# Windowed means of a pooling mixer: sliding sums on VectorE over turned token tiles, in place of TensorE products with band and edge matrices

## The chip, the cores and the metric

The kernel runs on one core of one Trainium2 chip. The metric is the time of one execution on the device, in microseconds (us); for each kernel it is the median of its runs.

## What is computed

The reference is a two-layer decoder trunk over 1040 tokens (16 meta tokens ahead of 1024) of width 1024. Layer 0 mixes tokens with sparse attention and a gated recurrence, layer 1 with a causal pooling mixer. Behind each mixer comes a layer norm, then a SwiGLU block of width 2816, then another layer norm. The change touches the pooling mixer alone. Cut to what matters:

```python
POOL_WINDOWS = (2, 4, 8, 16)            # one window per group of 256 features
def multiscale_pool(h, w_pool, scale):
    cs = cumulative sum of h over the tokens, with a zero ahead
    for g, w in enumerate(POOL_WINDOWS):
        lo  = max(pos + 1 - w, 0)
        mean = (cs_g[1:] - cs_g[lo]) / (pos + 1 - lo)
        outs.append((mean - h_g) @ w_pool[g])       # 256 x 256
    return concatenate(outs) * scale

h = layer_norm(ALPHA * h + mix)
h = layer_norm(ALPHA * h + swiglu(h))
```

The 16 meta tokens are dropped from the output, so every token that is stored has a full window behind it, and the mean of a window of w is its sum over w.

## The kernel before, in words

Three stages follow one another: `projection`, `mixers` and `trunk`. The trunk is the SwiGLU blocks, the norms and the pooling mixer, and the change lies in it. The token tiles are tile 0 (the 16 meta tokens) and tiles 1 to 8 (128 tokens each); they stay in SBUF as `y`, with tokens on the partitions.

The trunk runs four phases: layer 0 for tiles 0 to 4, layer 0 for tiles 5 to 8, layer 1 for tiles 1 to 4, layer 1 for tiles 5 to 8. A phase has 11 pairs; a pair handles two slices of 128 hidden features. For each pair g, TensorE's program is: `gate_up(2g)` (48 products with a moving size of 512, L2067), `down(g-1)` (8 groups of 6 products, L2101), `gate_up(2g+1)`. Each fp32 weight is split into a high and a low part: ACT makes the high part (`high_w` L2181, `high_d` L2187), POOL the low part (`low_w` L1978, `low_d` L1985), the SP queue loads the next slice when both are done (`load_w` L1912). VectorE does `gated` (the product with the gate L2292, then the low part of the hidden values L2302) behind each `gate_up`, and `add` (L2318) behind each group of `down`. `down` turns over three PSUM banks: group n waits for the `add` of group n-3.

The norms and the pooling mixer of layer 1 lie between these pieces, written out by hand: `steps_in` says which token tile is in which step T in which pair. Phase 1 does it for tiles 1 to 4, phase 2 for tiles 5 to 8; one tile per pair, in eight pairs. For pooled tile j (tile m = j + 1):

- step T = j + 4: between `gate_up(2g)` and `down(g-1)`, `pool_d` (L2106) makes the windowed mean less the token, already turned so that features lie on the partitions. Eight products of a piece of `y` with a 128 x 128 `band` matrix (L2115), and eight with an `edge` matrix that bring in the last tokens of the tile before (L2121 for the first tile, L2124 else). ACT and VectorE copy the two PSUM banks out to `dT` (`turned_d`, L2211 and L2326), which has two buffers.
- step T = j + 5: behind the next pair's `down`, `pool_mix` (L2128) multiplies `dT` with the pooling weights (L2137), and VectorE adds the result to `y` and takes the norm's statistics (`mix`, L2329).
- step T = j + 8: `n2.turn` (L1764) turns the normed tile with eight TensorE transposes, between two `gate_up`s.

POOL makes `band` and `edge` in pairs 3 to 6 (`bands`, L1990), and keeps the tail of tile 4 for phase 2 (L2032). It multiplies the pooling weights with `pool_scale` in pair 8 (L2022).

An engine does its own instructions in the order in which they are written, and waits at semaphores.

Of the kernel before, what the change touches and what calls it, by code (L numbers as in the profile page):

```python
# [9 lines left out]
ALU = mybir.AluOpType  # L10
ACT = mybir.ActivationFunctionType

P = 128
D = 1024
# [1801 lines left out]
def trunk(nc, c, sem, sb, banks, ident, ins, y, hH, hL, raw, draw, out):  # L1816
# [3 lines left out]
    TAIL = 32  # L1820
# [17 lines left out]
    band = sb(c, "band", [P, NW, P])  # L1838
    edge = sb(c, "band_edge", [P, NW, P])
    dT = sb(c, "dT", [P, 2, DC, P])  # L1840
    meta_rest = dT[:, 1, :, :].rearrange("p k t -> p (k t)")
    scale = dT[:, 0, :, :].rearrange("p k t -> p (k t)").rearrange("p (g f) -> p g f", g=NW)
# [6 lines left out]
    pool_loaded, w_ready, made, made_all = sem("pool_loaded"), sem("pool_w"), sem("band_made"), sem("bands_done")  # L1849
    d_psum, d_act, d_dve, mix_psum, mixed, kept = (sem("d_psum"), sem("d_act"), sem("d_dve"), sem("mix_psum"),  # L1850
                                                   sem("mixed"), sem("tail_kept"))
# [18 lines left out]
    BANDS_AT = {3: 0, 4: 1, 5: 2, 6: 3}  # L1870
# [98 lines left out]
    def _(pool):  # L1969
# [18 lines left out]
        made_count = [0]  # L1988

        def bands(g):  # L1990
            win = POOL_WINDOWS[g]
            for mat, r, base in ((band, slice(0, P), 0), (edge, slice(0, N_META), N_META), (edge, slice(P - TAIL, P), TAIL)):
                at = mat[r, g, :]
                nc.gpsimd.memset(at, 1.0 / win).then_inc(made, 1)
                made_count[0] += 1
                pool.wait_ge(made, made_count[0])
                nc.gpsimd.affine_select(out=at, in_=at, compare_op=ALU.is_gt, fill=0.0, base=win - base,
                                        pattern=[[-1, P]], channel_multiplier=1).then_inc(made, 1)
                made_count[0] += 1
                pool.wait_ge(made, made_count[0])  # L2000
                if base == 0:
                    nc.gpsimd.affine_select(out=at, in_=at, compare_op=ALU.is_ge, fill=0.0, base=0,
                                            pattern=[[1, P]], channel_multiplier=-1).then_inc(made, 1)
                    made_count[0] += 1
                    pool.wait_ge(made, made_count[0])
                    nc.gpsimd.tensor_tensor(at, at, ident[:, :], ALU.subtract).then_inc(made_all, 1)

# [3 lines left out]
        for g in range(NPAIR):  # L2011
# [5 lines left out]
            if g in BANDS_AT:  # L2017
                bands(BANDS_AT[g])
            if g == SCALE_AT:
                pool.wait_ge(pool_loaded, 32)  # L2020
                for k in range(2):
                    nc.gpsimd.tensor_tensor(w[:, :, k, :], w[:, :, k, :], scale, ALU.mult).then_inc(w_ready, 1)  # L2022
            if first_norm(ph, i, 2) is not None:
                n0.bias(pool, first_norm(ph, i, 2))
            for T, normed, pooled in steps_in(ph, i):
                if T - 7 in pooled:
                    n2.bias(pool, T - 7)
                if T - 2 in normed:
                    n1.bias(pool, T - 2)
                    if T - 2 == HALF:  # L2030
                        pool.wait_ge(n1.biased, HALF + 1)
                        nc.gpsimd.tensor_copy(y[P - TAIL:P, 0, :], y[P - TAIL:P, HALF, :]).then_inc(kept, 1)  # L2032
                        pool.wait_ge(kept, 1)
# [9 lines left out]
    def _(pe):  # L2043
# [61 lines left out]

        def pool_d(j):  # L2106
            m = j + 1
            pe.wait_ge(n1.biased, m + 1)
            if j == 0:
                pe.wait_ge(made_all, NW)  # L2110
                pe.wait_ge(made, 3 * 2 * NW + NW)
            if m == HALF + 1:
                pe.wait_ge(kept, 1)
            for k in range(DC):
                nc.tensor.matmul(banks[:, PB + k // 4, k % 4 * P:(k % 4 + 1) * P], y[:, m, k * P:(k + 1) * P], band[:, k // 2, :],  # L2115
                                 start=(k % 4 == 0), stop=False)
            for k in range(DC):
                at = banks[:, PB + k // 4, k % 4 * P:k % 4 * P + N_META]
                cols, g = slice(k * P, (k + 1) * P), k // 2
                if m == 1:  # L2120
                    last = nc.tensor.matmul(at, y[0:N_META, 0, cols], edge[0:N_META, g, 0:N_META], start=False, stop=(k % 4 == 3))  # L2121
                else:
                    prev = 0 if m == HALF + 1 else m - 1
                    last = nc.tensor.matmul(at, y[P - TAIL:P, prev, cols], edge[P - TAIL:P, g, 0:N_META],  # L2124
                                            start=False, stop=(k % 4 == 3))
            last.then_inc(d_psum, 1)

        def pool_mix(j, turned):  # L2128
# [3 lines left out]
            pe.wait_ge(d_dve, d_made[0])  # L2132
            if turned:
                pe.wait_ge(n2.lo, 2 * turned)
            for g in range(NW):
                for k in range(2):
                    last = nc.tensor.matmul(banks[:, PB + g // 2, g % 2 * PG:(g % 2 + 1) * PG],  # L2137
                                            dT[:, j % 2, 2 * g + k, :], w[:, g, k, :], start=(k == 0), stop=(k == 1))
# [37 lines left out]
    def _(act):  # L2176
# [27 lines left out]

        def turned_d(j):
            act.wait_ge(d_psum, j + 1)
            if j == 0:
                act.wait_ge(w_ready, 2)
            if j >= 2:
                act.wait_ge(mix_psum, j - 1)  # L2210
# [223 lines left out]
```

## Time and profile before

| | us |
|---|---|
| median of 3 runs | 2550.95 (2549.44 to 2551.99) |
| the profiled execution, its own time | 2547.58 |
| its span, first to last instruction | 2545.9 |
| TensorE matmuls busy (share of the span) | 2469.9 (97%) |
| VectorE busy | 1114.2 (44%) |
| ScalarE busy | 950.1 (37%) |
| GpSimd busy | 1062.1 (42%) |
| mean granted TensorE clock, of full speed | 0.992 |

In the profile PE is TensorE's matmuls, PEld its weight loads, DVE is VectorE, ACT ScalarE, POOL GpSimd and SP the queue that issues the loads. A timeline row gives an instruction's start and its duration from the span's start; a bracket at its end is the idle time of the engine ahead of it and what ended that. Neighbouring matmuls overlap in the record, so the cost of one is the distance between two starts, not its duration. An fp32 product that is not a transpose is two instructions in the trace; `x16` is eight products.

### The profile page before, as it was taken

What the parts mean: (1) busy time and instruction counts of PE and PEld (TensorE: products, weight loads), DVE (VectorE), ACT (ScalarE), POOL (GpSimd) and SP (SyncE); (2) the same over time, 40 slices, a digit from 0 to 9 for tenths busy, and PEclk for the clock granted to TensorE, in tenths of its full rate; (3) what the DMA queues carried; (4) which work ended last, traced back from release to release, by engine and by line L of the source; (5) the groups of instructions that cost most, each with busy time, mean ns of one, the idle gap of its engine ahead of it and who ended that gap; (6) DMA issues with size and microseconds to landing.
All of it is one profiled execution on the core that took longest, in us unless ns stands there. A gap on an engine that the chain in (4) does not pass through costs nothing.

```text
span 2545.9 us, 36095 instructions
## 1 busy us (share of the span) xinstructions
PE 2469.9 (97%) x14044; PEld 2129.0 (84%) x14044; DVE 1114.2 (44%) x2233; ACT 950.1 (37%) x1609; POOL 1062.1 (42%) x617
## 2 busy tenths in 40 slices
PE   7999999899999989999999999999999999999997
PEld 7889999768888778899898888888888888888885
DVE  7798986444554523333333332333323322232224
ACT  3687783334443224222223332323333322332222
POOL 1434213365554224444433544544434443455342
PEclk9999999899999999999999999999999999999998
DMA  4101230333332333333323323333233233333431
GB/s 139 34 18 56 79 103 24 108 112 110 113 106 90 93 116 109 96 96 105 89 74 99 99 75 93 88 112 97 70 99 100 67 116 99 100 89 110 116 94 47
DMA packets 275002, 231.43 MB, mean 91 GB/s; under 512 B 10768, under 2 KB 255568, under 8 KB 274832
## 3 DMA queue, kind: packets, MB, share of 16 engines
q1 hardware_dynamic: 266640, 220.59, 29.1%
q10 hardware_dynamic: 8192, 8.52, 1.0%
q8 instruction: 113, 1.85, 0.3%
q14 instruction: 57, 0.47, 0.1%
HBM read 215.81 MB, written 12.71 MB: 90 GB/s over the span
## 4 chain that ended last, share of the span: by engine, by line
PE 60%; ACT 1%; DVE 1%; DMA 1%; POOL 0%; issue 0%; POOLq 0%; SPq 0%; ACTq 0%; DVEq 0%
PE banks L2067 38%; PE banks L2101 19%; PE banks L2137 1%; PE banks L2115 1%; PE banks L1764 1%; PE banks L2124 1%; PE banks L2092 0%; PE banks L2095 0%; DMA last_draw<-in_w_down 0%; DMA cq_raw<-in_w_up 0%; POOL dL L1985 0%; POOL wL L1978 0%; DVE y L2318 0%; ACT dH L2187 0%; ACT hH L1774 0%
## 5 line engine op out<-in xcount | busy, mean ns | idle before, releaser
L1978 POOL TENSOR_TENSOR wL<-cq_raw,wH 128x2048 fp32r<-128x2048 f32 x87 | 407.0, 4678 | 531.5 <-ACT wH L2181 531.5
L2067 PE MATMUL banks<-hL,wH 128*128 128x512 f32 (+1 forms) x1760 | 618.7, 352 | 6.6 <-ACT hid L2196 3.8
L2067 PE MATMUL banks<-hH,wL 128*128 128x512 f32 (+1 forms) x1760 | 617.9, 351 | 0.0
L2067 PE MATMUL banks<-hH,wH 128*128 128x512 f32 (+1 forms) x1760 | 616.2, 350 | 0.0
L2292 DVE TENSOR_TENSOR hid<-hid,banks 128x512 f32<-128x512 f32 (+1 forms) x110 | 64.4, 585 | 729.4 <-PE banks L2067 629.0
L2067 PEld LDWEIGHTS banks<-hL,wH 128*128 128x128 f32 x1760 | 331.3, 188 | 55.8 <-ACT hid L2196 5.1
L2067 PEld LDWEIGHTS banks<-hH,wL 128*128 128x128 f32 x1760 | 331.2, 188 | 46.3
L2067 PEld LDWEIGHTS banks<-hH,wH 128*128 128x128 f32 x1760 | 331.8, 188 | 45.0
L1985 POOL TENSOR_TENSOR dL<-last_draw,dH 128x1024 fp32r<-128x1024 f32 x88 | 220.9, 2510 | 321.3 <-ACT dH L2187 321.2
L2318 DVE TENSOR_TENSOR y<-y,banks 128x512 f32<-128x512 f32 (+1 forms) x340 | 232.3, 687 | 195.0 <-PE banks L2101 194.0
L2187 ACT ACTIVATE dH<-last_draw 128x1024 fp32r<-128x1024 f32 x88 | 93.3, 1061 | 517.6 <-PE banks L2101 340.7
L2101 PE MATMUL banks<-dH,hidL 128*128 128x512 f32 x704 | 279.2, 397 | 2.3 <-issue 2.3
L2101 PE MATMUL banks<-dL,hidH 128*128 128x512 f32 x704 | 278.0, 395 | 0.0
L2101 PE MATMUL banks<-dH,hidH 128*128 128x512 f32 x704 | 277.5, 394 | 0.0
L2198 ACT ACTIVATE hidH<-hid 128x512 fp32r<-128x512 f32 (+1 forms) x110 | 60.4, 549 | 382.1 <-DVE hid L2292 382.1
L2181 ACT ACTIVATE wH<-cq_raw 128x2048 fp32r<-128x2048 f32 x87 | 166.0, 1908 | 40.1 <-DMA cq_raw<-in_w_up 37.8
L2101 PEld LDWEIGHTS banks<-dH,hidL 128*128 128x128 f32 x704 | 132.3, 188 | 35.0 <-issue 2.7
L2101 PEld LDWEIGHTS banks<-dH,hidH 128*128 128x128 f32 x704 | 132.6, 188 | 31.5
L1124 POOL TENSOR_TENSOR qp<-qp,tot 64x256 f32<-64x256 f32 x112 | 80.6, 720 | 186.9 <-PE banks L1289 182.5
L2101 PEld LDWEIGHTS banks<-dL,hidH 128*128 128x128 f32 x704 | 132.6, 188 | 30.5
L501 PE MATMUL banks<-shared,hH 128*128 128x256 f32 (+1 forms) x648 | 136.9, 280 | 0.0
L501 PE MATMUL banks<-shared,hL 128*128 128x256 f32 (+1 forms) x432 | 120.7, 280 | 0.0
(279 smaller groups left out, 4124.4 us busy)
## 6 DMA issues: line engine op xcount, KB each, us to landing
cq_raw<-in_w_gate SPq DMA_DIRECT2D x88, 512.0 KB, 4.5
cq_raw<-in_w_up SPq DMA_DIRECT2D x88, 512.0 KB, 6.0
last_draw<-in_w_down SPq DMA_DIRECT2D x88, 512.0 KB, 3.4
w_out_part<-in_w_out SPq DMA_DIRECT2D x60, 512.0 KB, 3.9
va<-in_w_in SPq DMA_DIRECT2D x10, 1024.0 KB, 5.4
va<-in_x SPq DMA_DIRECT2D x8, 512.0 KB, 4.3
vg_scratch<-y ACTq DMA_DIRECT2D x32, 128.0 KB, 1.7
y<-in_x SPq DMA_DIRECT2D x8, 512.0 KB, 7.5
```

The source lines that it names most:

```text
L501: last = nc.tensor.matmul(banks[0:n, bank, 0:SW], h[:, k, a:a + n], w[:, k, :], start=first, stop=stop)
L1124: nc.gpsimd.tensor_tensor(late, late, blocks[r, :, 0, :].to_broadcast([HD, n, 2 ** l]), ALU.mult)\
L1764: last = self.nc.tensor.transpose(self.banks[:, self.bank_of(i), k * P:k * P + n], self.y[0:n, m, kk * P:(kk + 1) * P], self.ident[0:n, 0:n])
L1978: nc.gpsimd.tensor_tensor(wL[:, ff % 2, :, :, :].rearrange("p g k f -> p (g k f)"), raw[:, :, :, :].rearrange("p g k f -> p (g k f)"), wH[ ...
L1985: nc.gpsimd.tensor_tensor(dL[:, ff % 2, :], draw, dH[:, ff % 2, :].bitcast(F32), ALU.subtract)\
L2067: last = nc.tensor.matmul(banks[:, GU + (2 * q + g) % 3, 0:n], wt[:, ff % 2, g, k, :], h[:, k, a:a + n], start=(k == 0 and part == 0), sto ...
L2101: last = nc.tensor.matmul(banks[0:n, DN + num % 3, :], h[:, (2 * g + u) % 3, t0 - ph.t0:t0 - ph.t0 + n], wt[:, u, (j % 2) * 512:(j % 2 + 1 ...
L2181: nc.scalar.activation(wH[:, ff % 2, :, :, :], raw[:, :, :, :], ACT.Copy).then_inc(w_hi, 2)
L2187: nc.scalar.activation(dH[:, ff % 2, :], draw, ACT.Copy).then_inc(d_hi, 1)
L2198: nc.scalar.activation(hidH[:, ff % 3, a - ph.t0:a - ph.t0 + n], hid[:, q % 2, 0:n], ACT.Copy)\
L2292: nc.vector.tensor_tensor(hid[:, q % 2, 0:n], hid[:, q % 2, 0:n], banks[:, GU + (2 * q + 1) % 3, 0:n], ALU.mult)\
L2318: nc.vector.tensor_tensor(at, at, banks[0:n, DN + num % 3, :], ALU.add).then_inc(y_added, 1)
```

## The change

`pool_d` now only turns the tile: eight transposes with the identity in place of sixteen products. Its result, `xT`, holds each feature's 128 tokens with 16 columns ahead of them for the tokens before. VectorE makes the sums of 2, 4, 8 and 16 tokens there, each from the one before (`sums`), into `dT`, which is one buffer now and shares `pool_work` with the scale. The sum of w less w times the token goes into the product; the 1/w is put on the pooling weights by way of `pool_scale` (four ACT steps in pair 7). `sums(j)` stands at the end of its pair on VectorE, behind `gated(2g+1)`, and ends with a copy of the tile's last 16 columns to the front of `xT`. The meta tile is turned once (`turn_meta`), ahead of the first pooled pair's `gate_up`. The bands, the edges and POOL's copy of the tail are gone. The walk with a step of -1 makes each column from columns that are not yet overwritten.

```diff
-    dT = sb(c, "dT", [P, 2, DC, P])
+    xT = sb(c, "xT", [P, DC, N_META + P])
+    work = sb(c, "pool_work", [P, 2 * D])
+    dT = work[:, 0:DC * (N_META + P)].rearrange("p (k t) -> p k t", k=DC)
+    meta_rest = work[:, D:2 * D]
+    scale = work[:, 0:D].rearrange("p (g f) -> p g f", g=NW)
...
+        def turn_meta():
+            pe.wait_ge(n1.biased, 1)
+            for k in range(DC):
+                last = nc.tensor.transpose(banks[:, PB, k * N_META:(k + 1) * N_META], y[0:N_META, 0, k * P:(k + 1) * P],
+                                           ident[0:N_META, 0:N_META])
+            last.then_inc(meta_psum, 1)
+
         def pool_d(j):
             m = j + 1
             pe.wait_ge(n1.biased, m + 1)
             if j == 0:
-                pe.wait_ge(made_all, NW)
-                pe.wait_ge(made, 3 * 2 * NW + NW)
-            if m == HALF + 1:
-                pe.wait_ge(kept, 1)
+                pe.wait_ge(meta_xT, 1)
             for k in range(DC):
-                nc.tensor.matmul(banks[:, PB + k // 4, k % 4 * P:(k % 4 + 1) * P], y[:, m, k * P:(k + 1) * P], band[:, k // 2, :],
-                                 start=(k % 4 == 0), stop=False)
-            for k in range(DC):
-                at = banks[:, PB + k // 4, k % 4 * P:k % 4 * P + N_META]
-                cols, g = slice(k * P, (k + 1) * P), k // 2
-                if m == 1:
-                    last = nc.tensor.matmul(at, y[0:N_META, 0, cols], edge[0:N_META, g, 0:N_META], start=False, stop=(k % 4 == 3))
-                else:
-                    prev = 0 if m == HALF + 1 else m - 1
-                    last = nc.tensor.matmul(at, y[P - TAIL:P, prev, cols], edge[P - TAIL:P, g, 0:N_META],
-                                            start=False, stop=(k % 4 == 3))
+                last = nc.tensor.transpose(banks[:, PB + k // 4, k % 4 * P:(k % 4 + 1) * P], y[:, m, k * P:(k + 1) * P],
+                                           ident[:, :])
             last.then_inc(d_psum, 1)
...
+            pe.wait_ge(d_ready, j + 1)
...
+            if any(T == 4 and 0 in pooled for T, normed, pooled in steps):
+                turn_meta()
             gate_up(2 * g)
...
+        def turned_meta():
+            act.wait_ge(meta_psum, 1)
+            nc.scalar.activation(xT[:, :, 0:N_META], banks[:, PB, 0:DC * N_META].rearrange("p (k t) -> p k t", k=DC), ACT.Copy)\
+              .then_inc(meta_xT, 1)
...
+            if g == SCALE_AT - 1:
+                act.wait_ge(pool_loaded, 32)
+                for k, window in enumerate(POOL_WINDOWS):
+                    nc.scalar.activation(scale[:, k, :], scale[:, k, :], ACT.Copy, scale=1.0 / window).then_inc(averaged, 1)
...
             dve.wait_ge(d_psum, j + 1)
-            if j == 0:
+            if j:
+                dve.wait_ge(tail_kept, j)
+            nc.vector.tensor_copy(xT[:, 4:8, N_META:], banks[:, PB + 1, :].rearrange("p (k t) -> p k t", k=4))\
+              .then_inc(d_dve, 1)
+        def sums(j):
+            dve.wait_ge(d_act, j + 1)
+            dve.wait_ge(d_dve, j + 1)
+            if j:
+                dve.wait_ge(mix_psum, j)
+            else:
                 dve.wait_ge(w_ready, 2)
-            if j >= 2:
-                dve.wait_ge(mix_psum, j - 1)
-            nc.vector.tensor_copy(dT[:, j % 2, 4:8, :], banks[:, PB + 1, :].rearrange("p (k t) -> p k t", k=4))\
-              .then_inc(d_dve, 1)
+                dve.wait_ge(unfolded, 1)
+                dve.wait_ge(meta_xT, 1)
+            now = xT[:, :, N_META:]
+            nc.vector.tensor_tensor(dT[:, 0:CG, N_META:], xT[:, 0:CG, N_META - 1:-1], now[:, 0:CG], ALU.subtract)
+            nc.vector.tensor_tensor(dT[:, CG:, 2:], xT[:, CG:, 2:], xT[:, CG:, 1:-1], ALU.add).then_inc(summed, 1)
+            for g in range(1, NW):
+                back = 2 ** g
+                dve.wait_ge(summed, NW * j + g)
+                at, before = dT[:, CG * g:, 2 * back:], dT[:, CG * g:, back:-back]
+                nc.vector.tensor_tensor(at[:, :, ::-1], at[:, :, ::-1], before[:, :, ::-1], ALU.add).then_inc(summed, 1)
+            dve.wait_ge(summed, NW * j + NW)
+            for g in range(1, NW):
+                at = slice(CG * g, CG * (g + 1))
+                last = nc.vector.scalar_tensor_tensor(out=dT[:, at, N_META:], in0=now[:, at], scalar=-float(POOL_WINDOWS[g]),
+                                                      in1=dT[:, at, N_META:], op0=ALU.mult, op1=ALU.add)
+            last.then_inc(d_ready, 1)
+            if j + 1 < 2 * HALF:
+                dve.wait_ge(d_ready, j + 1)
+                nc.vector.tensor_copy(xT[:, :, 0:N_META], xT[:, :, P:P + N_META]).then_inc(tail_kept, 1)
...
-            if j == HALF - 1:
-                dve.wait_ge(kept, 1)
-            elif m + 1 < NT:
-                dve.wait_ge(d_psum, j + 2)
...
                     n2.low(dve, T - 8)
+                if T - 4 in pooled:
+                    sums(T - 4)
```

On TensorE, around `pool_d` of the second pooled tile, before (L2067 is `gate_up`, L2101 `down`):

```order
L2067 MATMUL banks<-hH,wH 128x512
L2115 MATMUL banks<-band,y 128x128 x8
L2124 MATMUL banks<-band_edge,y 128x16 x8
L2101 MATMUL banks<-dH,hidL 128x512
L2101 MATMUL banks<-dL,hidH 128x512
L2101 MATMUL banks<-dH,hidH 128x512
```

and with the change (L2095 is the transpose, L2077 `down`):

```order
L2043 MATMUL banks<-hH,wH 128x512
L2095 MATMUL banks<-ident,y 128x128 x8
L2077 MATMUL banks<-dH,hidL 128x512
L2077 MATMUL banks<-dL,hidH 128x512
L2077 MATMUL banks<-dH,hidH 128x512
```

Of the sixteen products ahead of `down` eight transposes are left. This is so for each of the eight pooled tiles.

On VectorE, from the end of the first pooled pair to the adds of `down` in the next, before (L2292 and L2302 are `gated`, L2326 `turned_d`, L2318 `add`):

```order
L2302 TENSOR_TENSOR hidL<-hid,hidH 128x512
L2292 TENSOR_TENSOR hid<-hid,banks 128x512
L2302 TENSOR_TENSOR hidL<-hid,hidH 128x512
L2326 COPY dT<-banks 128x512
L2318 TENSOR_TENSOR y<-y,banks 128x512 x8
```

and with the change (L2275 and L2285 are `gated`, L2307 `turned_d`, L2301 `add`):

```order
L2285 TENSOR_TENSOR hidL<-hid,hidH 128x512
L2321 TENSOR_TENSOR pool_work<-xT 128x2x128
L2322 TENSOR_TENSOR pool_work<-xT 128x6x142
L2327 TENSOR_TENSOR pool_work<-pool_work 128x6x140
L2327 TENSOR_TENSOR pool_work<-pool_work 128x4x136
L2327 TENSOR_TENSOR pool_work<-pool_work 128x2x128
L2331 SCALAR_TENSOR_TENSOR pool_work<-xT,pool_work 128x2x128 x3
L2336 COPY xT<-xT 128x8x16
L2275 TENSOR_TENSOR hid<-hid,banks 128x512
L2285 TENSOR_TENSOR hidL<-hid,hidH 128x512
L2307 COPY xT<-banks 128x4x128
L2301 TENSOR_TENSOR y<-y,banks 128x512 x8
```

Nine instructions have come in between the `gated` at a pair's end and the `gated` of the next pair. `pool_work` is `dT`.

## Rows read from the trace of the kernel before

**Rows 1.** The page: busy time; the chain that ended last, by engine

```profile
PE 2469.9 (97%) x14044; PEld 2129.0 (84%) x14044; DVE 1114.2 (44%) x2233; ACT 950.1 (37%) x1609; POOL 1062.1 (42%) x617
...
PE 60%; ACT 1%; DVE 1%; DMA 1%; POOL 0%; issue 0%; POOLq 0%; SPq 0%; ACTq 0%; DVEq 0%
```

**Rows 2.** Phases 1 and 2: length, busy time per engine (count), clock, DMA

```profile
1412.00:2010.00 598.00, 598.00 (x2732) 491.60 (x2732) 192.25 (x316) 191.17 (x196) 266.82 (x80) 1.00 0.31 92
```

**Rows 3.** Timeline of TensorE, first and second tile's windows (start, length, operation)

```profile
1424.80 1.95 PE L2115 MATMUL banks<-band,y 128*128 128x128 f32 x16
...
1462.05 1.95 PE L2115 MATMUL banks<-band,y 128*128 128x128 f32 x16
1463.92 1.95 PE L2124 MATMUL banks<-band_edge,y 32*128 32x16 f32 x16
...
1466.14 0.39 PE L2101 MATMUL banks<-dL,hidH 128*128 128x512 f32 x1
```

**Rows 4.** Groups of TensorE by form (count | busy, mean ns)

```profile
L2124 PE MATMUL banks<-band_edge,y 32*128 32x16 f32 x112 | 13.7, 259 | 0.0
```

**Rows 5.** Timeline of TensorE at the turn of a normed tile

```profile
1609.74 1.03 PE L1764 MATMUL banks<-ident,y 128*128 128x128 f32 x8
...
1610.84 0.39 PE L2067 MATMUL banks<-hH,wL 128*128 128x512 f32 x1
```

**Rows 6.** Timeline of TensorE at the trunk's start: sixteen turns in a row

```profile
949.68 1.91 PE L1764 MATMUL banks<-ident,y 128*128 128x128 f32 x16
951.35 0.37 PE L2067 MATMUL banks<-hL,wH 128*128 128x264 f32 x1
```

**Rows 7.** Timeline of POOL: the biases of tiles 0 and 1

```profile
1407.12 5.83 POOL L1743 TENSOR_TENSOR y<-y,n_b 16x1024 f32<-16x1024 f32 x2
```

**Rows 8.** Timeline of VectorE in phase 1 (idle before and its releaser in brackets)

```profile
1462.31 0.69 DVE L2292 TENSOR_TENSOR hid<-hid,banks 128x512 f32<-128x512 f32 x1 [9.01 <-PE banks L2067]
...
1573.22 0.69 DVE L2292 TENSOR_TENSOR hid<-hid,banks 128x512 f32<-128x512 f32 x1 [8.15 <-PE banks L2067]
...
1584.34 0.69 DVE L2292 TENSOR_TENSOR hid<-hid,banks 128x512 f32<-128x512 f32 x1 [9.04 <-PE banks L2067]
1585.73 0.69 DVE L2302 TENSOR_TENSOR hidL<-hid,hidH 128x512 fp32r<-128x512 f32 x1 [0.70 <-ACT hidH L2198]
1586.34 0.68 DVE L2318 TENSOR_TENSOR y<-y,banks 128x512 f32<-128x512 f32 x1
```

**Rows 9.** Groups of VectorE ahead of the trunk, by form

```profile
L720 DVE SCALAR_TENSOR_TENSOR found<-found 128x1 int32<-128x1 int32 x90 | 29.0, 322 | 0.0
...
L742 DVE MATCH_REPLACE8 y<-top,y 128x528 f32<-128x528 f32 x32 | 22.0, 688 | 0.0
...
L742 DVE MATCH_REPLACE8 y<-top,y 128x400 f32<-128x400 f32 x18 | 10.0, 553 | 0.0
...
L775 DVE TENSOR_TENSOR_SCAN search_rows<-search_rows 128x1040 f32<-128x1040 f32 x1 | 2.3, 2326 | 0.0
```

**Rows 10.** Timeline of VectorE: a 512-column step, then a dependent one

```profile
1523.29 0.68 DVE L1674 BATCH_NORM_STATS2 n_bn<-y 128x6 f32<-128x512 f32 x1
1524.00 0.21 DVE L1676 BATCH_NORM_AGGREGATE n_mv<-n_bn 128x2 f32<-128x12 f32 x1
```

**Rows 11.** Timeline of POOL in the same stretch

```profile
1576.52 4.67 POOL L1978 TENSOR_TENSOR wL<-cq_raw,wH 128x2048 fp32r<-128x2048 f32 x1 [6.68 <-ACT wH L2181]
1589.04 4.68 POOL L1978 TENSOR_TENSOR wL<-cq_raw,wH 128x2048 fp32r<-128x2048 f32 x1 [7.84 <-ACT wH L2181]
```

**Rows 12.** Timelines of POOL and VectorE where both read SBUF

```profile
1370.52 2.41 POOL L1985 TENSOR_TENSOR dL<-last_draw,dH 128x1024 fp32r<-128x1024 f32 x1 [5.24 <-ACT dH L2187]
...
1371.63 2.37 DVE L2361 TENSOR_TENSOR y<-y,dT 16x1024 f32<-16x1024 f32 x1 [1.62 <-ACT dT L2235]
```

**Rows 13.** Busy time and clock at the trunk's start, and behind a turn

```profile
946.40:949.70 3.30, 3.30 (x17) 3.30 (x17) 0.00 (x0) 0.00 (x0) 0.70 (x1) 0.50 1.13 308
1610.60:1620.00 9.40, 9.40 (x43) 7.65 (x42) 2.08 (x4) 4.01 (x5) 4.69 (x1) 1.00 0.05 13
```

More of the change, by code:

```diff
@@ L1837, in trunk @@
     w = sb(c, "w_pool_sb", [P, NW, 2, PG])
-    band = sb(c, "band", [P, NW, P])
-    edge = sb(c, "band_edge", [P, NW, P])
-    dT = sb(c, "dT", [P, 2, DC, P])
-    meta_rest = dT[:, 1, :, :].rearrange("p k t -> p (k t)")
-    scale = dT[:, 0, :, :].rearrange("p k t -> p (k t)").rearrange("p (g f) -> p g f", g=NW)
+    xT = sb(c, "xT", [P, DC, N_META + P])
[3 more added lines that the diff above has]
+    scale = work[:, 0:D].rearrange("p (g f) -> p g f", g=NW)
+    CG = DC // NW
+    assert max(POOL_WINDOWS) == N_META and list(POOL_WINDOWS) == [2 ** (g + 1) for g in range(NW)]
     raw_loaded, draw_loaded = sem("raw_loaded"), sem("draw_loaded")
@@ L1848, in trunk @@
     down_psum, y_added = sem("down_psum"), sem("y_added")
-    pool_loaded, w_ready, made, made_all = sem("pool_loaded"), sem("pool_w"), sem("band_made"), sem("bands_done")
-    d_psum, d_act, d_dve, mix_psum, mixed, kept = (sem("d_psum"), sem("d_act"), sem("d_dve"), sem("mix_psum"),
-                                                   sem("mixed"), sem("tail_kept"))
+    pool_loaded, w_ready, averaged = sem("pool_loaded"), sem("pool_w"), sem("pool_scale_averaged")
+    d_psum, d_act, d_dve, mix_psum, mixed = (sem("d_psum"), sem("d_act"), sem("d_dve"), sem("mix_psum"), sem("mixed"))
+    meta_psum, meta_xT, summed, d_ready, tail_kept = (sem("meta_turned"), sem("meta_xT"), sem("window_sums"), sem("d_ready"),
+                                                      sem("tail_kept"))
     stored, gain_kept = sem("stored"), sem("gain_kept")
@@ L1986, in low_d @@
               .then_inc(d_lo, 1)
[L1988 to L2006, printed above, removed]
         low_w(0)
@@ L2016, in _ @@
                 low_d(2 * g)
-            if g in BANDS_AT:
-                bands(BANDS_AT[g])
             if g == SCALE_AT:
+                pool.wait_ge(averaged, NW)
                 pool.wait_ge(pool_loaded, 32)
@@ L2137, in pool_mix @@
                     last = nc.tensor.matmul(banks[:, PB + g // 2, g % 2 * PG:(g % 2 + 1) * PG],
-                                            dT[:, j % 2, 2 * g + k, :], w[:, g, k, :], start=(k == 0), stop=(k == 1))
+                                            dT[:, CG * g + k, N_META:], w[:, g, k, :], start=(k == 0), stop=(k == 1))
             last.then_inc(mix_psum, 1)
@@ L2224, in _ @@
             steps = steps_in(ph, i)
+            if any(T == 4 and 0 in pooled for T, normed, pooled in steps):
+                turned_meta()
             gated(2 * g)
@@ L2321, in turned_d @@
             dve.wait_ge(d_psum, j + 1)
[L2322 to L2327 removed]
+            if j:
[5 more added lines that the diff above has]
+            dve.wait_ge(d_dve, j + 1)
+            if j:
+                dve.wait_ge(mix_psum, j)
+            else:
+                dve.wait_ge(w_ready, 2)
+                dve.wait_ge(unfolded, 1)
[17 more added lines that the diff above has]
+                nc.vector.tensor_copy(xT[:, :, 0:N_META], xT[:, :, P:P + N_META]).then_inc(tail_kept, 1)
         def mix(j):
```

13 lines of the change are left out of this document (2 added, 11 removed).

## Prediction

> **What bounds the kernel now.** The first view is the page [rows 1]. TensorE's matmuls are busy for 97% of the span, VectorE for 44%, GpSimd for 42%; the chain that ended last is 60% TensorE and 1% VectorE. A share of a whole span can hide a stretch with another limit, so the second view is the busy time of the stretch that holds all pooled tiles, phases 1 and 2 [rows 2]: of 598.00 us TensorE is busy 598.00, at a granted clock of 1.00, and VectorE 192.25. TensorE never waits there. What is taken off its program shortens the run one for one, until something else ends later; what is put on another engine costs nothing, until TensorE waits for it. So two questions decide: how much leaves TensorE, and whether the new steps on VectorE end in time.
>
> **What leaves TensorE.** The third view is TensorE's timeline at a tile's windows [rows 3]. The eight band products begin at 1462.05, the eight edge products at 1463.92, and the second product of `down` at 1466.14: 4.09 us. The edge products bring in 16 columns each, yet they cost as much as the full ones (1.9 us a tile; [rows 4] has seven tiles' worth of them). The same piece with eight transposes instead stands in the trace where a normed tile is turned [rows 5]: first transpose at 1609.74, second product of `gate_up` behind them at 1610.84, 1.10 us. The products around both are of one size, so the difference is the price: 4.09 - 1.10 = 2.99 us a tile, eight tiles, **23.9 us less**.
>
> The transposes of the meta tile are new on TensorE, once. Sixteen transposes took 951.35 - 949.68 = 1.67 us [rows 6]; eight take 0.84, and I take that for 16 columns too, since the edge products above did not get cheaper with 16 columns. **0.8 us more**, and not below zero. They wait for tile 0's bias. POOL begins the two biases at 1407.12 and is through both 5.83 us later [rows 7], so at 1412.95. A `gate_up` takes 1584.34 - 1573.22 = 11.12 us [rows 8], and the first tile's band products began at 1424.80 [rows 3], so the `gate_up` behind the new transposes began at 1413.7. No wait, with 0.8 us to spare for both biases and more for the one that is needed. ACT's copy of the result has the whole `gate_up` to be made in.
>
> POOL loses the bands, the edges and the tail copy, ACT gains nine small steps. TensorE does not wait for either in this stretch [rows 2], and POOL, which made the bands in phase 0, has 0% of the chain [rows 1]. Both count as nothing.
>
> TensorE's sum is 0.84 - 23.9 = **-23.1 us**.
>
> **What VectorE gets, and whether it is hidden.** `sums` handles 256 + 852 + 840 + 544 + 256 columns in five steps of two tensors, 3 x 256 in three more, and copies 128: 3644 columns in nine instructions. Price of a column: a walk over 528 columns took 688 ns and one over 400 took 553 [rows 9], so 1.05 ns; the 400 are walked backwards, as three of the new steps are, and are not dearer. Price of an instruction: one of 512 columns began 0.61 us ahead of the next (1585.73 and 1586.34 [rows 8]), so 0.07 us besides the columns; where the next one waits for the result it is 0.71 [rows 10], 0.10 more. Five of the nine wait so. S = 3644 x 1.05 + 9 x 0.07 + 5 x 0.10 = **5.0 us**.
>
> They stand in a gap: behind the hidden values' low part, VectorE is idle for 9.04 us until `gate_up` has ended [rows 8]; this gap is there behind all eight pooled tiles. But POOL makes the low part of the weights in that gap, from 1576.52 for 4.67 us [rows 11], and both read SBUF. That shows in two rows [rows 12]: VectorE's add of two SBUF tensors came at 1371.63 into a POOL subtraction that ran from 1370.52 to 1372.93, and ended at 1374.00, one full add of 1.07 us behind POOL's end. One engine stood still until the other was through. So I count S and POOL's 4.67 us one behind the other: 9.67 in a gap of 9.04, and the next `gated` is late by x = S - 4.37 = 0.6 us.
>
> How late may it be? Take the old start of that product (1584.34 [rows 8]) as zero. TensorE goes on 0.26 ahead of it (1462.05 [rows 3] against 1462.31 [rows 8]). The eight transposes take 1.10 less 0.23 for the product behind them (11.12 / 48), so to +0.61, and three groups of `down` (six products, 1.39 each) to +4.78. There it needs the first `add`. On VectorE the low part begins 1.39 behind the product and the next instruction 0.61 behind that [rows 8]; with the copy out of the bank (0.61) and the add itself (0.69), the first add ends at x + 3.30. TensorE waits from x = 1.48, so from **S = 5.85**. The forecast has 0.85 us a tile to spare and no wait. Behind the two tiles whose next pair has no transposes the limit is 0.3 lower, still above.
>
> If instead VectorE keeps POOL waiting, the weights' low part ends up to 5 us later, and so does the next load. The next low part began at 1589.04 [rows 11] and would begin at 1594; it ends at 1599, for a `gate_up` that begins behind 1610 [rows 5]. It is hidden by 11 us.
>
> Bounds of S. Below: 3.8 us, the columns alone. Above: the dearest row per column is a scan, 2326 ns for 1040 columns, 2.24 each, and a step of one column that waits for the one before took 322 ns [rows 9]: 3644 x 2.24 + 5 x 0.32 = 9.8 us. The plain adds are nearest to the row of 512 columns, so I take 5.0.
>
> One rule speaks against the change. The clock was at its full 2.4 GHz (granted 1.00) in the 9.4 us behind the eight transposes of a normed tile [rows 5, 13]. The Trainium skill (TensorE: Matmul & The Clock Gate, Part 4) says that a transpose does not count as busy time for the clock as a matmul does. By that rule each tile would risk a dip, and the sum would be that of the second rival below in place of -23.1. I go by the row, by which the clock costs nothing.
>
> **Sum.** The profiled execution took 2547.58, so 2524.5 with the change. The median of the runs shown is 3.4 us above that execution, and the median is what is forecast: 2550.95 - 23.1 = **2527.9 us**.
>
> **The rivals.**
> - *VectorE's steps are somewhat dearer and TensorE waits a little.* Walks with a step of -1 over rows of 144 columns are not in the trace in just this form. If the three backward steps (1640 columns) went at half speed, S = 5.0 + 1.7 = 6.7, a wait of 0.85 a tile, 6.8 us in all: 2534.7. For it: only 0.85 us of room. Against it: the backward walk [rows 9].
> - *The clock dips behind the transposes.* At the trunk's start, behind turns and a wait, the clock was 0.50 (1.2 GHz) for 3.3 us [rows 13], which lost half of that. Eight times 1.65 is 13.2 us: 2541.1. Against it: the full clock behind the turn of a normed tile.
> - *VectorE's columns cost what the scan's cost.* S = 3644 x 2.24 + 5 x 0.10 = 8.65, a wait of 2.8 a tile, 22.4 us: 2550.2, no change.
> - *Slower.* The wait for `add` in `down` becomes TensorE's bound in every pooled pair. A tile's wait is S - 5.85; it cancels the gain at S = 8.74 and costs over 5.1 us from S = 9.4 on. At the upper bound of 9.8 it is 3.95 a tile, 31.6 us: 2559.4. For it: SBUF shared with POOL, and five steps in a chain. Against it: plain adds would have to cost double.
> - *The gain is not there*, since another engine ends later: excluded for the most part, as the same pairs run without windows at the weights' pace, with TensorE at 598.00 of 598.00.
>
> **Chances.** Forecast 0.76; dearer steps 0.12; clock 0.04; scan's price or no gain 0.05; slower 0.03. A measurement of this kernel can tell about 0.2% (5.1 us) from no change. Faster by more than that: 0.92. Within: 0.05. Slower: 0.03. The range is 2524.5 (the profiled execution's own sum) to 2536 (the first rival at its stated size, and the scatter of the runs, 1 us); the clock, the scan and the slower case stay outside, with the far half of the first.
>
> **What would show it.** Right: TensorE's distance from the first transpose to the second product of `down` is 1.10 us, for eight tiles; phases 1 and 2 have TensorE without idle time and a clock of 1.00; nine steps of VectorE start to end in some 9.7 us, POOL's 4.67 among them; VectorE's next product is late by 0.6 us. Wrong: idle time of TensorE released by VectorE's `add` in `down`; a granted clock below 1.00 behind transposes; an add of 840 columns over 1.1 us where POOL is at rest.

## The result, and the profile after

| | before | after |
|---|---|---|
| median (4 runs each, on one chip) | 2550.26 (2549.44 to 2551.99) | 2524.45 (2523.23 to 2525.57) |
| ratio, 95% interval | | 0.9898 (0.9882 to 0.9913) |
| the profiled execution, its own time | 2547.58 | 2525.57 |
| its span | 2545.9 | 2523.8 |
| mean granted TensorE clock | 0.992 | 0.991 |

The changed kernel is faster by 25.8 us, about 1.0%; the interval of the ratio reaches from 22 to 30 us. The prediction had 23.1 us and a time of 2527.9. The direction and the size of the mechanism were right, as the next rows show; the time lies 0.05 us below the range, which began at 2524.5. Where that comes from is the first question behind the rows. One run of the kernel before, in a later set, took 5268.89 us, twice the time; it is left out of every figure.

The page of the changed kernel, busy time and the chain that ended last:

```profile
PE 2448.3 (97%) x13860; PEld 2107.5 (84%) x13860; DVE 1185.3 (47%) x2304; ACT 951.8 (38%) x1614; POOL 1053.6 (42%) x584
...
PE 60%; DMA 1%; ACT 1%; POOL 1%; DVE 1%; issue 0%; POOLq 0%; SPq 0%; ACTq 0%; DVEq 0%
```

Against [rows 1] TensorE is busy for 21.6 us less and VectorE for 71.1 us more, and VectorE's part of the chain is 1% as before. What VectorE got is hidden.

Phases 1 and 2 by the view of stretches (length, busy time and instructions of PE, PEld, DVE, ACT, POOL, then the clock), which answers to [rows 2]:

```profile
1412.00:1988.00 576.00, 576.00 (x2552) 470.02 (x2551) 263.57 (x388) 192.60 (x199) 268.83 (x80) 1.00 0.33 96
```

TensorE is still without idle time and at a clock of 1.00. To measure what the phases take, I use the distance between two of VectorE's products with the gate that stand ahead of and behind all eight pooled tiles (the 48th and the 80th of the trunk): 596.00 us before

```profile
1413.94 0.69 DVE L2292 TENSOR_TENSOR hid<-hid,banks 128x512 f32<-128x512 f32 x1 [3.98 <-ACT hid L2196]
...
2009.94 0.69 DVE L2292 TENSOR_TENSOR hid<-hid,banks 128x512 f32<-128x512 f32 x1 [8.17 <-PE banks L2067]
```

and after

```profile
1416.31 0.69 DVE L2275 TENSOR_TENSOR hid<-hid,banks 128x512 f32<-128x512 f32 x1 [3.98 <-PE banks L2043]
...
1989.08 0.69 DVE L2275 TENSOR_TENSOR hid<-hid,banks 128x512 f32<-128x512 f32 x1 [8.14 <-PE banks L2043]
```

572.77 us. That is **23.23 us less**, where the sum on TensorE had been 23.1.

TensorE's timeline at a pooled tile and, first, at the meta tile (to set beside [rows 3] and [rows 5]):

```profile
1415.82 0.39 PE L2043 MATMUL banks<-hH,wH 128*128 128x512 f32 x1
1416.14 0.66 PE L2085 MATMUL banks<-ident,y 16*128 16x16 f32 x8
1416.73 0.51 PE L2043 MATMUL banks<-hL,wH 128*128 128x512 f32 x1
...
1462.19 1.04 PE L2095 MATMUL banks<-ident,y 128*128 128x128 f32 x8
1462.98 0.47 PE L2077 MATMUL banks<-dH,hidL 128*128 128x512 f32 x1
1463.30 0.39 PE L2077 MATMUL banks<-dL,hidH 128*128 128x512 f32 x1
```

From the first transpose to the second product of `down`: 1.11 us (4.09 before). The meta tile's turn made the distance between the gate products around it 11.93 us, where it was 11.13: 0.80 us, so eight tiles gave 24.03, 3.00 each.

VectorE behind the same tile, which answers to the idle 9.04 us of [rows 8]:

```profile
1451.52 0.69 DVE L2275 TENSOR_TENSOR hid<-hid,banks 128x512 f32<-128x512 f32 x1 [7.60 <-ACT hid L2170]
1452.91 0.69 DVE L2285 TENSOR_TENSOR hidL<-hid,hidH 128x512 fp32r<-128x512 f32 x1 [0.70 <-ACT hidH L2172]
1453.52 0.42 DVE L2321 TENSOR_TENSOR pool_work<-xT 128x256 f32<-128x256 f32 x1
1453.86 1.04 DVE L2322 TENSOR_TENSOR pool_work<-xT 128x852 f32<-128x852 f32 x1
1454.93 6.68 DVE L2327 TENSOR_TENSOR pool_work<-pool_work 128x840 f32<-128x840 f32 x3
1461.64 1.10 DVE L2331 SCALAR_TENSOR_TENSOR pool_work<-xT,pool_work 128x256 f32<-128x256 f32 x3
1462.78 0.23 DVE L2336 COPY xT<-xT 128x128 f32<-128x128 f32 x1
1462.92 0.68 DVE L2275 TENSOR_TENSOR hid<-hid,banks 128x512 f32<-128x512 f32 x1
```

POOL in the same stretch:

```profile
1454.83 4.67 POOL L1979 TENSOR_TENSOR wL<-cq_raw,wH 128x2048 fp32r<-128x2048 f32 x1 [2.77 <-ACT wH L2155]
```

The nine steps begin at 1453.52 and the product behind them at 1462.92: 9.40 us, where 9.67 was forecast. That product comes 11.40 us behind the one before it, and TensorE does not wait. In the row of L2327 `x3` stands for three backward adds, of 840, 544 and 256 columns.

### The profile page after: what moved, and what is told of

Same layout as the page of the kernel before. It is cut to its first block, busy times and chain, and to the rows that moved or that the text cites. A ratio compares the mean times of both kernels' runs of the same rounds, so it can differ in the third digit from the quotient of the medians.

```text
span 2523.8 us, 35771 instructions
## 1 busy us (share of the span) xinstructions
PE 2448.3 (97%) x13860; PEld 2107.5 (84%) x13860; DVE 1185.3 (47%) x2304; ACT 951.8 (38%) x1614; POOL 1053.6 (42%) x584
## 4 chain that ended last, share of the span: by engine, by line
PE 60%; DMA 1%; ACT 1%; POOL 1%; DVE 1%; issue 0%; POOLq 0%; SPq 0%; ACTq 0%; DVEq 0%
PE banks L2043 38%; PE banks L2077 19%; PE banks L2109 1%; PE banks L1764 1%; DMA last_draw<-in_w_down 0%; PE banks L2068 0%; PE banks L2071 0%; POOL dL L1986 0%; PE banks L2095 0%; DMA cq_raw<-in_w_up 0%; POOL wL L1979 0%; ACT dH L2161 0%; DVE y L2301 0%; ACT hH L1774 0%; DVE n_bn L1673 0%
## 5 line engine op out<-in xcount | busy, mean ns | idle before, releaser
L2275 DVE TENSOR_TENSOR hid<-hid,banks 128x512 f32<-128x512 f32 (+1 forms) x110 | 64.3, 584 | 657.7 <-PE banks L2043 552.0
L2301 DVE TENSOR_TENSOR y<-y,banks 128x512 f32<-128x512 f32 (+1 forms) x340 | 232.1, 686 | 181.5 <-PE banks L2077 180.3
L2077 PE MATMUL banks<-dH,hidL 128*128 128x512 f32 x704 | 278.3, 395 | 2.3 <-issue 2.3
L2077 PE MATMUL banks<-dL,hidH 128*128 128x512 f32 x704 | 277.3, 394 | 0.0
L2077 PE MATMUL banks<-dH,hidH 128*128 128x512 f32 x704 | 276.9, 393 | 0.0
L2077 PEld LDWEIGHTS banks<-dH,hidL 128*128 128x128 f32 x704 | 132.0, 188 | 34.5 <-issue 2.7
L2077 PEld LDWEIGHTS banks<-dH,hidH 128*128 128x128 f32 x704 | 132.2, 188 | 31.2
L2077 PEld LDWEIGHTS banks<-dL,hidH 128*128 128x128 f32 x704 | 132.3, 188 | 30.4
```

The costliest lines, as they stand in the source:

```text
L2077: last = nc.tensor.matmul(banks[0:n, DN + num % 3, :], h[:, (2 * g + u) % 3, t0 - ph.t0:t0 - ph.t0 + n], wt[:, u, (j % 2) * 512:(j % 2 + 1 ...
L2275: nc.vector.tensor_tensor(hid[:, q % 2, 0:n], hid[:, q % 2, 0:n], banks[:, GU + (2 * q + 1) % 3, 0:n], ALU.mult)\
L2301: nc.vector.tensor_tensor(at, at, banks[0:n, DN + num % 3, :], ALU.add).then_inc(y_added, 1)
```

## The experiments

All ratios are to the kernel before, on the same chip and in the same set of runs, with 95% intervals. There were three such sets, each on a chip of its own: the changed kernel again, the run without edge products, and those with one and with four extra steps; then the kernel before again, the two runs without POOL, and that with two steps; last the run with three. So medians of different sets are not to be compared to the microsecond, but ratios and phases are. "Phases" is the distance between the two gate products.

### Is the result more than the sum? The two kernels once more

The changed kernel again, and in a later set of runs the kernel before against itself. No edit in either.

> The changed kernel once more. Its profiled execution has, from one TensorE product to the same one, 23.2 us less than before across phases 1 and 2, and nothing else that the change made; the medians shown differ by 25.8. Theory A: the change is worth 23.2 us and the other 2.6 are scatter of the runs (stretches of 3.4 us at half clock, one more or one less at places with idle time that both kernels have). Then five more rounds give a difference from before of 22 to 25 us. Theory B: the change is worth 26 us, by something that the two profiles hide. Then it is 25.5 us or more again.

> The kernel before once more, for the size of the scatter by itself. Theory A (the runs scatter by stretches at half clock that come or stay away at places with idle time): from one TensorE product to the same one in phases 1 and 2 its profile agrees with the first one within 0.2 us, and what differs, by 1 to 4 us, lies ahead of the trunk, at its start or behind the last wait at its end, beside another list of stretches at half clock. Rival: the phases themselves differ by a microsecond or more, and the 23.2 us read from them is not exact.

Measured: the changed kernel 2527.23 us (2523.87 to 2529.70, 5 runs), ratio 0.9909 (0.9896 to 0.9922), which is 23 us less, with an interval from 20 to 27 (the medians of this set differ by 21.3). Theory A's 22 to 25 us hold the ratio's figure, but the interval does not shut out theory B's 25.5; what speaks for A is the phases. Its phases took 572.77 us again, the same to the hundredth. The kernel before against itself: 2549.97 us (2545.73 to 2551.72, 10 runs), ratio 0.9998 (0.9988 to 1.0007), phases 596.00, the same as in the first profile.

So the stretch that the change touches repeats exactly, and the rest does not. All 50 runs of the kernel before have a median of 2549.80 and spread from 2545.73 to 2553.82; all nine of the changed one have 2525.09, from 2523.23 to 2529.70. The medians differ by 24.7 us. What moves a single run shows in its mean granted clock: the five runs of the changed kernel above had 0.989, 0.989, 0.991, 0.992 and 0.992 with spans of 2527.9, 2526.6, 2525.4, 2522.1 and 2522.7. In the profile these are short stretches at 1.2 GHz, all outside the two phases. Two of them in the changed kernel's second profile, and that profile's phases:

```profile
921.80:925.10 3.30, 3.30 (x9) 2.59 (x8) 0.29 (x1) 0.00 (x0) 0.00 (x0) 0.52 0.00 0
...
2498.80:2502.10 3.30, 3.30 (x9) 2.59 (x9) 0.69 (x1) 0.69 (x1) 0.00 (x0) 0.53 0.00 0
1412.00:1988.00 576.00, 576.00 (x2552) 470.01 (x2551) 266.17 (x392) 193.82 (x200) 271.16 (x81) 1.00 0.33 96
```

Whether one comes differs between two profiles of the changed kernel, where the program is the same: the stretch at 2498.80 above, at the last `down`, is missing in the first. In the profile of before:

```profile
2516.00:2519.60 3.60, 3.30 (x8) 2.65 (x9) 0.64 (x2) 1.77 (x2) 0.00 (x0) 0.55 0.00 0
```

and in that of after:

```profile
2495.00:2498.70 3.70, 3.25 (x14) 2.73 (x15) 1.25 (x3) 1.91 (x3) 0.00 (x0) 1.00 0.00 0
```

In the first pair of profiles the spans differ by 22.1 us: 23.23 less in the phases, 1.2 less behind them (this row), 2.4 more ahead of them, where TensorE's program is the same. One rival stays open here. The stretch at the last `down` is in both profiles of the kernel before (535.94 us from the second gate product to the end, both times) and in that of the run without edge products, but in only three of the eight profiles of kernels with the change, extra steps included: in the two here those last parts are 534.70 and 536.27 us. Whether the change makes it rarer, which would be worth some 0.6 us more in the mean (an estimate from these eleven profiles), so few cannot tell.

### What the edge products cost alone

The kernel before without its eight edge products. It leaves out, in the windows, the tokens of the tile before.

```diff
             for k in range(DC):
-                nc.tensor.matmul(banks[:, PB + k // 4, k % 4 * P:(k % 4 + 1) * P], y[:, m, k * P:(k + 1) * P], band[:, k // 2, :],
-                                 start=(k % 4 == 0), stop=False)
-            for k in range(DC):
...
-                    last = nc.tensor.matmul(at, y[P - TAIL:P, prev, cols], edge[P - TAIL:P, g, 0:N_META],
-                                            start=False, stop=(k % 4 == 3))
+                last = nc.tensor.matmul(banks[:, PB + k // 4, k % 4 * P:(k % 4 + 1) * P], y[:, m, k * P:(k + 1) * P], band[:, k // 2, :],
+                                 start=(k % 4 == 0), stop=(k % 4 == 3))
```

> The kernel before, with the eight edge products of each tile left out (so a window that reaches into the tile before is cut off there) and nothing else. Theory A: these products of 16 columns cost TensorE 1.88 us a tile, 15.0 us in all, though they bring in an eighth of the columns: 2535 to 2536 against 2550.5, two thirds of the change's gain. Rival: a product of 16 columns is mostly cheap, its record is long only since TensorE's records overlap: then under 6 us.

Measured: 2533.85 us (2532.16 to 2536.76, 5 runs), ratio 0.9942 (0.9930 to 0.9954). Phases 579.45, 16.55 less than before: 2.07 us a tile. TensorE's timeline at that tile:

```profile
1461.10 1.95 PE L2115 MATMUL banks<-band,y 128*128 128x128 f32 x16
1462.80 0.48 PE L2101 MATMUL banks<-dH,hidL 128*128 128x512 f32 x1
1463.12 0.40 PE L2101 MATMUL banks<-dL,hidH 128*128 128x512 f32 x1
```

and the two gate products:

```profile
1415.08 0.69 DVE L2283 TENSOR_TENSOR hid<-hid,banks 128x512 f32<-128x512 f32 x1 [3.98 <-PE banks L2067]
...
1994.53 0.69 DVE L2283 TENSOR_TENSOR hid<-hid,banks 128x512 f32<-128x512 f32 x1 [8.17 <-PE banks L2067]
```

What follows: of the 3.00 us of a tile, 2.07 were the edges and 0.93 the bands' exchange for transposes. The eight edge products with 16 moving columns are not cheaper than the eight of the bands with 128: those take 1.79 us by the rows above (1463.12 - 1461.10, less 0.23 for the product behind them). This part alone would have brought seven tenths of the gain. The expectation had 1.88 us a tile, 15.0 in all.

### POOL and VectorE in one gap

In the changed kernel, POOL makes only 8 columns of the weights' low part in the pairs behind a pooled tile (the low part of those eight slices is left out), so that VectorE has SBUF to itself.

```diff
+        def low_w_first(ff):
+            pool.wait_ge(w_hi, 2 * ff + 2)
+            nc.gpsimd.tensor_tensor(wL[:, ff % 2, 0, 0, 0:8], raw[:, 0, 0, 0:8], wH[:, ff % 2, 0, 0, 0:8].bitcast(F32), ALU.subtract)\
+              .then_inc(w_lo, 2)
...
             if 2 * g + 3 < NFF:
-                low_w(2 * g + 3)
+                if any(T - 4 in pooled for T, normed, pooled in steps_in(ph, i)):
+                    low_w_first(2 * g + 3)
+                else:
+                    low_w(2 * g + 3)
```

> The changed kernel, with POOL's subtraction of 2048 columns behind each pooled tile cut to 8 columns (the low part of eight weight slices is left out). Theory A (SBUF is read by one of the two engines at a time): the step of 840 columns takes 1.0 us in place of 4.9, the nine steps 4.7 us end to end in place of 9.4, and VectorE stands idle for 4 us behind them; the time stays the changed kernel's within 1 us, since nobody waited. Rival: the step of 840 columns is dear by its backward walk: it stays over 2 us.

Measured: 2528.52 us (2523.72 to 2531.37, 4 runs), ratio 0.9906 (0.9890 to 0.9923). Phases 572.77, as with the change. VectorE behind the tile:

```profile
1457.73 0.42 DVE L2329 TENSOR_TENSOR pool_work<-xT 128x256 f32<-128x256 f32 x1
1458.06 1.04 DVE L2330 TENSOR_TENSOR pool_work<-xT 128x852 f32<-128x852 f32 x1
1459.14 2.25 DVE L2335 TENSOR_TENSOR pool_work<-pool_work 128x840 f32<-128x840 f32 x3
1461.42 1.10 DVE L2339 SCALAR_TENSOR_TENSOR pool_work<-xT,pool_work 128x256 f32<-128x256 f32 x3
1462.56 0.23 DVE L2344 COPY xT<-xT 128x128 f32<-128x128 f32 x1
1466.71 0.69 DVE L2283 TENSOR_TENSOR hid<-hid,banks 128x512 f32<-128x512 f32 x1 [3.92 <-PE banks L2051]
```

The copy is followed by the next instruction 0.14 us behind its start (1462.78 and 1462.92 above), so the nine steps take 1462.56 + 0.14 - 1457.73 = 4.97 us; S had been put at 5.0. The three backward adds take 2.25 us here and 6.68 beside POOL. The first of them, of 840 columns, in the groups of phases 1 and 2 (busy us, mean ns, idle before), in the changed kernel:

```profile
L2327 DVE TENSOR_TENSOR pool_work<-pool_work 128x840 f32<-128x840 f32 x8 | 39.2, 4906 | 0.3
```

and in this one:

```profile
L2335 DVE TENSOR_TENSOR pool_work<-pool_work 128x840 f32<-128x840 f32 x8 | 8.3, 1033 | 0.3
```

The mean of 4906 ns is over unlike tiles: at seven of the eight this add takes 5.45 to 5.48 us, and at the fifth 1.03. There VectorE's add began 0.19 us ahead of POOL's subtraction, which took 5.39 us in place of 4.67, and the next add, of 544 columns, took 5.08 in place of 0.73. So the engine that begins first holds up the other. Behind the first tile it is POOL, and VectorE stands for 4.43 of POOL's 4.67 us, nearly as the prediction had it from [rows 12]: 4.97 + (6.68 - 2.25) = 9.40, as measured. The Trainium skill (SBUF — State Buffer, Who interferes with whom) calls the pair of ports that these engines share an exclusive lock, and says that an operation of VectorE with two SBUF inputs contends with one of GpSimd that reads SBUF; the two rows agree.

### How much room there is: one, two, three and four steps more

The changed kernel with n extra adds of 896 columns per pooled tile, each behind the one before, ahead of the last sums. They compute nothing that is used.

```diff
+            for i in range(n):
+                if i or j:
+                    dve.wait_ge(extra, n * j + i)
+                nc.vector.tensor_tensor(spare, old, old, ALU.add).then_inc(extra, 1)
             dve.wait_ge(summed, NW * j + NW)
```

> The changed kernel with one more step of VectorE in each of the eight sums: an add of two SBUF tensors of 896 columns into columns that nothing reads, 1.1 us. The nine steps take 4.7 us in the changed kernel's trace, so S = 5.8 and the product behind them is 1.4 us late. Theory A: TensorE waits from S = 5.85 on, so the time is the changed kernel's within 0.5 us, and VectorE's product comes 1.1 us later than there. Rival: the room is smaller, since something else waits for VectorE too: then up to 8.8 us more.

> The changed kernel with two added steps, 2.2 us a tile: S = 6.95. Four steps gave waits of 3.0 us for VectorE's add and, behind each, 3.4 or 6.8 us at half clock. Theory A: TensorE waits S - 5.85 - 0.3 = 0.8 us a tile, 7 us in all, and so short a wait does not lower the clock: 2531 to 2533. Rival: every wait for VectorE lowers the clock: 13 us more, 2545.

> The changed kernel with three extra adds of 896 columns per pooled tile, each behind the one before, ahead of the last sums; nothing is left out. With two of them VectorE's next product was late by 2.43 us and TensorE stood for 0.92 us a tile, for 0.99 us of time; with four it was late by 4.70 and TensorE stood for 3.14, for 4.64 us of time, of which the clock took 1.7. With three the product is late by 2.43 + 1.13 = 3.56, and TensorE should stand for 3.56 - 1.5 = 2.05 us a tile. Theory A (a wait of 2 us costs itself and 0.1 us, as the one of 0.9 did, and the granted clock stays at 1.00): phases 1 and 2 are 8 x 2.15 = 17.2 us longer than with the change, ratio to before about 0.997, faster than before by some 6 to 8 us. Theory B (behind a wait of 2 us the clock falls too, for 3.4 us each time): 8 x (2.15 + 1.7) = 30.8 us longer, ratio about 1.003, slower than before by some 7 us. Shown by the distance between VectorE's gate products no. 48 and 80 and the granted clock behind the waits.

> The same with four such steps, 4.4 us a tile: S = 9.2. Theory A: TensorE waits S - 5.85 = 3.3 us a tile (3.6 for two of them) for the first add of `down`, 27 us in all, so 2551 to 2552: the whole gain is gone. Rival: the waits are taken up elsewhere, or VectorE's share of the SBUF lock is paid once only: then under 10 us more than the changed kernel.

And four of them with POOL out of the way, as in the experiment above:

> The same with the four added steps of VectorE (4.4 us a tile), which cost 37 us where POOL subtracts. Theory A: without POOL in the gap of 9.0 us S = 9.2 us fits but for 0.2 us, under the room of 1.5: no wait of TensorE, 2524 to 2527 us. Rival: VectorE's 9.2 us are what counts, whoever else reads: 2560 again.

Measured. "Late" is, behind the first pooled tile, how much further than the 10.97 us of the run without POOL VectorE's next product comes behind the one before it; "stands" is TensorE's distance to the product that waited in `down` of the second tile, less the 0.23 us of an undisturbed one; "longer" is the phases against 572.77.

| extra steps | late, us | TensorE stands, us a tile | phases longer, us | median (runs) | ratio to before |
|---|---|---|---|---|---|
| 0 | 0.43 | none | 0 | 2527.23 (5) | 0.9909 (0.9896 to 0.9922) |
| 1 | 1.30 | none | 0.09 | 2526.16 (4) | 0.9907 (0.9893 to 0.9920) |
| 2 | 2.43 | 0.92 | 7.90 | 2532.66 (4) | 0.9931 (0.9916 to 0.9945) |
| 3 | 3.56 | 2.11 | 23.12 | 2549.61 (10) | 1.0000 (0.9991 to 1.0010) |
| 4 | 4.70 | 3.14 | 37.10 | 2564.28 (6) | 1.0060 (1.0047 to 1.0073) |
| 4, POOL's low part left out | 0.26 | none | 0 | 2528.81 (4) | 0.9911 (0.9896 to 0.9926) |

Behind the other tiles the product is less late: with the change alone 0.20 to 0.29 us at tiles 2 to 7 and not at all at tile 8, by the same comparison. TensorE begins to stand between x = 1.30 and 1.51 (2.43 - 0.92); the prediction had 1.48. With one extra step 0.07 of the 0.09 us lie in the `down` behind the fourth tile, one of the two for which the prediction had put the limit 0.3 lower; the product is late by 1.16 there. The last row shows that it is the sum of the steps and of POOL's 4.67 us that counts, and not the steps: the 4.4 us of four steps are free once POOL's are gone.

The expectations for one and for two steps held, in the phases, and so did theory A for four steps without POOL, though the median of its runs came out above the 2524 to 2527 forecast. The one for four steps beside POOL did not hold: it had 27 us of waits and 2551 to 2552, and the phases grew by 37.10.

TensorE's waits in phases 1 and 2, by the view of waits (us in total, times, longest us), with two extra steps:

```profile
PE banks L2080 <- DVE y L2304: 5.5, 8, 0.9
```

with three:

```profile
PE banks L2080 <- DVE y L2304: 14.6, 8, 2.0
```

and with four:

```profile
PE banks L2080 <- DVE y L2304: 23.5, 8, 3.2
```

It is the wait that the slower rival named: `down` for VectorE's `add`. But it costs more than itself. Even where the clock stays at 1.00, the product behind the one that waited comes 0.34 us behind it in place of 0.23, so each wait costs 0.1 more than it lasts. TensorE's timeline with four steps:

```profile
1467.15 0.40 PE L2080 MATMUL banks<-dH,hidH 128*128 128x512 f32 x1
1470.52 0.80 PE L2080 MATMUL banks<-dH,hidL 128*128 128x512 f32 x1 [2.97 <-DVE y L2304]
1471.11 0.63 PE L2080 MATMUL banks<-dL,hidH 128*128 128x512 f32 x1
1471.54 0.63 PE L2080 MATMUL banks<-dH,hidH 128*128 128x512 f32 x1
1471.96 0.63 PE L2080 MATMUL banks<-dH,hidL 128*128 128x512 f32 x1
```

Behind the wait the products stand 0.43 us apart in place of 0.23. The granted clock in the stretch from 1470.50 on is 0.50, and so it is behind some of the waits with three steps; with two it never falls. Stretches by the same view as above, with four steps:

```profile
1470.50:1473.40 2.90, 2.88 (x7) 2.31 (x8) 1.16 (x2) 0.33 (x1) 2.43 (x1) 0.50 0.00 0
```

with three, behind the waits that end at 1467.78 and at 1547.28:

```profile
1468.20:1471.20 3.00, 3.00 (x15) 2.41 (x14) 1.72 (x4) 0.00 (x0) 2.97 (x1) 1.00 0.00 0
1548.20:1551.20 3.00, 3.00 (x8) 2.30 (x7) 0.91 (x2) 0.00 (x0) 3.00 (x1) 0.50 0.00 0
```

and with two, both phases:

```profile
1412.00:1990.00 578.00, 572.46 (x2526) 464.66 (x2525) 277.93 (x402) 189.38 (x197) 264.81 (x79) 1.00 0.32 94
```

With three steps four of the eight waits are followed by a stretch of 3.4 us at 0.50. Set product by product beside the changed kernel, the eight waits come to 15.9 us, the products right behind them to 0.9, and the four stretches to 6.2, 1.55 each: 23.0 of the 23.12. With four steps six of the eight are followed by one or two such stretches, 27.3 us in all. The eight waits come to 24.9 us, and the other 12.2 are what the clock and the products right behind the waits cost. Four of these stretches begin while TensorE still waits, and that part loses nothing. Neither theory of the run with three steps was right: not without a dip, and not one at each wait, but one at half of them. What makes the difference between one wait of 2 us and the next stays open. A row of before could have warned of it: the stretch at 0.50 in [rows 13], at 946.40, came behind this wait of TensorE.

```profile
945.12 0.39 PE L2067 MATMUL banks<-hL,wH 128*128 128x264 f32 x1 [2.68 <-DVE hL L1783]
```

## Why the prediction was right or wrong

- **What leaves TensorE** was right: 3.00 us a tile (2.99 forecast), 0.80 for the meta tile (0.84), 23.23 in all (23.1). The price of products with 16 columns, which rested on a row of before alone, was borne out when they were taken away (2.07 us a tile, where the prediction had 1.9).
- **What hides VectorE's steps** was right in each term: S = 4.97 (5.0), one behind the other with POOL, late by 0.43 behind the first tile and by 0.3 or less behind the others (0.6), and room to 1.3 to 1.5 (1.48). The 0.2 us too much behind the first tile are POOL's 4.67, of which VectorE felt 4.43.
- **The backward adds** run at full rate, 1033 ns for 840 columns, against 1040 for the forward add of 852. The first rival (half speed), and the scan's price, are gone.
- **The clock behind the transposes** stayed at 1.00 in both phases, in both profiles of the changed kernel. The page of the Trainium skill that was weighed against the trace (TensorE: Matmul & The Clock Gate, Part 4) was rightly set aside for this case: eight transposes between products for 0.8 us were not followed by a dip in any of the eight tiles. Whether a longer row of them would be, no run here shows.
- **POOL, ACT and the queues** counted as nothing, and were nothing: TensorE is at 576.00 of 576.00.
- **The step that failed is the range's low end.** It was "the profiled execution's own sum", 2524.5, that is one execution's time less the change, with no room below it for scatter, though the three runs of before lay 1.0 and 1.5 us either side of their median, and the range's high end was given 1 us for it. The term was the scatter, and it was mis-sized: single runs of one kernel lie up to 4 us either side of their median (2545.73 to 2553.82 in 50 runs), and in the profiles what differs is stretches at 1.2 GHz outside the changed phases. The median of four such runs came out at 2524.45. In the second set the same kernel had 2527.23, within 0.7 us of the forecast of 2527.9, and 23.23 less than the 2549.80 of all runs of before is 2526.6, within the range. Of the 3.45 us between the forecast and the first median, 1.15 lie in its base, the median of only three runs (2550.95), 0.1 in the sum, and 2.1 in the scatter of the four runs after. That the second set came so near the forecast is therefore luck in part. Of the first difference of 25.8 us, 23.2 are shown to be the change; the other 2.6 lie within the interval, and the second set did not repeat them.
- **The slower rival was priced too low.** It had the gain cancelled at S = 8.74, by waits alone. The run with three extra steps is late by 3.13 us more than the change alone, so it has S = 4.97 + 3.13 = 8.1, and it is level with the kernel before: a tile costs 2.0 us of wait, where S - 5.85 gives 2.25, and 0.9 more for the product behind it and the clock, for which the prediction had nothing. The distance from the forecast of 5.0 to the point of no gain was 3.1 us, not 3.7; still far from what the steps took.

## What to carry to other kernels

Where one engine is busy all through a stretch, the distance between two fixed instructions around that stretch measures a change to some hundredths of a microsecond, while whole runs scatter by several; give the range of a predicted median that scatter on both sides. Work that moves to an idle engine is free up to a wait that can be worked out from before's timeline, if what GpSimd does in the same gap is counted in full. Past that point it costs more than the waits, since the clock falls behind some of them.

## What the runs showed of the hardware

- Eight fp32 products with 16 moving columns cost 2.07 us, no less than eight with 128 (1.79); eight fp32 transposes cost 0.88 us (1.11 less 0.23 for the product behind them), and 0.80 for 16 x 16 pieces.
- Waits of TensorE of 0.9 us leave the granted clock at 1.00; of eight waits of 2 us, four were followed by 3.4 us at 0.50; of eight of 3 us six, with 27.3 us at 0.50 in all. By the view of waits those last eight are 23.5 us; they cost 37.1.
- A VectorE add of two SBUF tensors that meets a GpSimd subtraction took 5.45 to 5.48 us at seven tiles where it takes 1.03 alone; at the one tile where the add began first, the subtraction took 5.39 us where it takes 4.67.
- The same instructions in untouched stages can differ by 2.6 us between runs of one kernel: the trunk's first gate product came at 955.92 and 958.53 us in two profiles of the kernel before.
